# Sample attention with the keys as the stationary operand

## The reference

```python
s = (jnp.einsum('bqhl,bkl->bhqk', q_lat, ckv, preferred_element_type=jnp.float32)
     + jnp.einsum('bqhr,bkr->bhqk', q_pe, kpe, preferred_element_type=jnp.float32))
s = jnp.where(mask, s * MLA_SCALE, NEG_INF)
p = jax.nn.softmax(s, axis=-1).astype(ckv.dtype)
return jnp.einsum('bhqk,bkl->bqhl', p, ckv)
```

## Time and profile before

| what | us |
|---|---|
| median of three timed executions | 4370.94 |
| the profiled execution | 4382.27 |
| its span | 4380.6 |
| PE busy in the span | 3606.5 |
| `mla_sample`, first layer (792 to 1279) | 487 |
| `mla_sample`, second layer (2946 to 3428) | 482 |

### The profile page before, as it was taken

How to read it: one execution, slowest core, us unless ns; L and a number is a source line. 1 busy time by engine, 2 the same in 40 slices (tenths; PEclk the granted TensorE clock), 3 DMA queues, 4 the chain that set the end, 5 groups by cost and what they waited for, 6 DMA issues and landing times. The chain is left out here.

```text
span 4380.6 us, 51760 instructions
## 1 busy us (share of the span) xinstructions
PE 3606.5 (82%) x20008; PEld 3033.2 (69%) x20008; DVE 1946.7 (44%) x3586; ACT 909.6 (21%) x1552; POOL 309.5 (7%) x366
## 2 busy tenths in 40 slices
PE   6974688566688999999999557875677889999997
PEld 4632466455577999999856234654555879999996
DVE  2453666333343544544451646652333344454443
ACT  2013233222221211111111032321222121111112
POOL 2000000222200000000010000003222000000000
PEclk9986799788898999999999658987898999999999
DMA  4111100333310111111121101004222111111111
GB/s 91 25 23 28 28 4 1 99 96 96 94 41 21 54 44 44 58 38 50 24 43 31 28 8 28 4 21 127 89 78 73 39 41 49 44 59 40 49 34 51
DMA packets 227424, 207.29 MB, mean 47 GB/s; under 512 B 51252, under 2 KB 196788, under 8 KB 227012
## 3 DMA queue, kind: packets, MB, share of 16 engines
q1 hardware_dynamic: 200584, 119.11, 10.1%
q0 software_dynamic: 26624, 85.11, 6.7%
HBM read 193.31 MB, written 11.05 MB: 47 GB/s over the span
## 5 line engine op out<-in xcount | busy, mean ns | idle before, releaser
L185 PE MATMUL ps<-streamH,upH 128*128 128x344 f32 x2112 | 451.4, 322 | 36.0 <-DVE streamL L2041 29.7
L185 PE MATMUL ps<-streamH,upL 128*128 128x344 f32 x2112 | 449.1, 321 | 0.0
L185 PE MATMUL ps<-streamL,upH 128*128 128x344 f32 x2112 | 447.6, 320 | 0.0
L185 PEld LDWEIGHTS ps<-streamH,upH 128*128 128x128 f32 x2112 | 356.0, 189 | 40.7 <-issue 34.7
L173 PE MATMUL ps<-hc,wring 128*128 128x344 f32 (+1 forms) x1248 | 366.5, 457 | 21.0 <-DVE hc L410 21.0
L1570 PE MATMUL ps<-kH,qpart 128*128 128x512 f32 x256 | 137.7, 538 | 287.5 <-DVE kL L1682 183.2
L185 PEld LDWEIGHTS ps<-streamH,upL 128*128 128x128 f32 x2112 | 357.7, 189 | 0.0
L185 PEld LDWEIGHTS ps<-streamL,upH 128*128 128x128 f32 x2112 | 354.3, 189 | 0.0
L173 PEld LDWEIGHTS ps<-hc,wring 128*128 128x128 f32 (+1 forms) x1248 | 230.3, 185 | 156.1 <-issue 44.2
L2088 DVE TENSOR_TENSOR xT<-xT,ps 128x1032 f32<-128x1032 f32 x176 | 216.1, 1229 | 240.2 <-PE ps L185 240.2
L1982 ACT ACTIVATE upH<-hc 128x1024 fp32r<-128x1024 f32 x88 | 93.3, 1062 | 981.1 <-PE ps L185 981.1
(11 more groups left out here) (423 smaller groups left out, 5603.1 us busy)
## 6 DMA issues: line engine op xcount, KB each, us to landing
hc<-in_w_ffn_in SPq DMA_DIRECT2D x88, 512.0 KB
hc<-in_w_ffn_out SPq DMA_DIRECT2D x44, 512.0 KB
wring<-in_w_in SPq DMA_DIRECT2D x22, 512.0 KB, 3.9
stream_raw<-in_w_out SPq DMA_DIRECT2D x16, 512.0 KB, 3.9
big<-in_x_prompt SPq DMA_DIRECT2D x1, 4096.0 KB
out_y_prompt<-big SPq DMA_DIRECT2D x8, 512.0 KB
scratch_y<-hc SPq DMA_DIRECT2D x16, 136.0 KB
scratch_u<-wring SPq DMA_DIRECT2D x4, 516.0 KB
```

The costliest lines, as they stand in the source:

```text
L185: last = pe.matmul(self.ps[:, bank + n, 0:NCOL], w, x[:, n * NCOL:(n + 1) * NCOL], start=(k == 0 and i == 0), stop=(k == len(terms) - 1 an ...
```

## The change

`mla_sample` is written anew. Gathers bring the same pages into the same two slots, but a group is now the 1024 keys of four samples, in two halves of the samples by turns; there are 16 groups a layer as before. The latents are still transposed (`latent`), now evicted once as plain fp32, by ACT for even and DVE for odd tiles, into four buffers `KT_`. In `scores` the transposed keys are the stationary operand and the sample's eight query columns move, so that scores stand with keys on the partitions: 128 partitions by 256 columns (sample, tile of keys, head). Rotary scores have 32 moving columns (`rotary_scores`), with the rotary rows transposed straight from `RB`. The softmax runs over 128 lanes, (sample, one of four tiles, head), each with its own running maximum and sum: PE turns the scores (`turned`), DVE takes the maximum along each lane, PE spreads its negative over all partitions by a product with ones (`lowered`), DVE adds it and ACT takes the exponential in place of keys (`pT`). In `values` the rows of `KB` are stationary and eight columns of `pT` move; ACT copies the result, and PE turns it back and sums the probabilities (`back`). After the last group the lanes are merged by their maxima with selecting products. Loops over groups are unrolled in the code of every engine. The sample's own row is handled as a lane of its own. Of the diff, lines that are removed, buffers, the start and the merge are left out here.

```diff
+        def place(g):
+
+            n, z = g // 2, g % 2
+            return n % 2, n // 2, [4 * z + i for i in range(4)]
+
+        def lanes(c, i, j=None):
+            a = c * P + i * 32
+            return slice(a, a + 32) if j is None else slice(a + 8 * j, a + 8 * j + 8)
...
+                for n in range(GATHERS):
+                    slot = n % 2
...
+                        if n >= 2:
+                            g = 2 * (n - 2) + b // 4
+                            pool.wait_ge(f_v, 4 * g + b % 4 + 1)
+                        at = bass.IndirectOffsetOnAxis(self.idx_i[:, n, b:b + 1].bitcast(U32), 0)
                         pool.indirect_dma_start(KB[slot][b], None, ckv_rows, at).then_inc(f_k[slot][b], 16)
                         pool.indirect_dma_start(RB[slot][:, b, :], None, krope_rows, at).then_inc(f_k[slot][b], 16)
...
+                def rotary(g, r):
+                    slot, turn, samples = place(g)
+                    for b in samples[2 * r:2 * r + 2]:
+                        pe.wait_ge(f_k[slot][b], 32 * turn + 32)
+                    if g or r:
+                        pe.wait_ge(f_rte, 2 * g + r)
+                    for x in range(4):
+                        b, c = samples[2 * r + x // 2], x % 2
+                        last = pe.transpose(ps[:, 3, x * P:(x + 1) * P], RB[slot][:, b, c * P:(c + 1) * P], ident)
+                    last.then_inc(f_rt, 1)
+
+                def latent(g, q):
+                    slot, turn, samples = place(g)
+                    b, c, at = samples[q // 2], q % 2, 8 * g + q
+                    pe.wait_ge(f_k[slot][b], 32 * turn + 32)
+                    if at >= KBANKS:
+                        pe.wait_ge(f_ke[(at - KBANKS) % 2], (at - KBANKS) // 2 + 1)
+                    for j in range(4):
+                        last = pe.transpose(ps[:, at % KBANKS, j * P:(j + 1) * P], KB[slot][b][:, (4 * c + j) * P:(4 * c + j + 1) * P], ident)
+                    last.then_inc(f_kt, 1)
+
+                def rotary_scores(g):
+                    samples = place(g)[2]
+                    pe.wait_ge(f_rte, 2 * g + 2)
+                    if g >= 2:
+                        pe.wait_ge(f_sc, g - 1)
+                    for i in range(4):
+                        for c in range(2):
+                            keys = rtb[g % 2][:, (2 * i + c) * P:(2 * i + c + 1) * P]
+                            last = pe.matmul(ps[:, 4 + g % 2, lanes(c, i)], keys, qrb[:, samples[i] * 32:samples[i] * 32 + 32],
+                                             start=(i == 0 and c == 0), stop=False)
+                    last.then_inc(f_rs, 1)
+
+                def scores(g, q):
+                    i, c, at = q // 2, q % 2, 8 * g + q
+                    b = place(g)[2][i]
+                    pe.wait_ge(f_ke[at % 2], at // 2 + 1)
+                    for j in range(4):
+                        last = pe.matmul(ps[:, 4 + g % 2, lanes(c, i, j)], KT_[at % KBUFS][:, j * P:(j + 1) * P], q_of(b),
+                                         start=False, stop=(q == 7 and j == 3))
+                    last.then_inc(f_s, 1)
+
+                def turned(g):
+                    pe.wait_ge(f_sc, g + 1)
+                    if g >= 2:
+                        pe.wait_ge(f_oc, g - 1)
+                    for c in range(2):
+                        last = pe.transpose(ps[:, 6, c * P:(c + 1) * P], raw[g % 2][:, c * P:(c + 1) * P], ident)
+                    last.then_inc(f_mt, 1)
+
+                def lowered(g):
+                    pe.wait_ge(f_dg, g + 1)
+                    pe.matmul(ps[:, 6, 0:P], ones, diag[g % 2], start=True, stop=True).then_inc(f_nm, 1)
+
+                def values(g, i):
+                    slot, _, samples = place(g)
+                    if i == 0:
+                        pe.wait_ge(f_p, g + 1)
+                        if g >= 1:
+                            pe.wait_ge(f_oe, g)
+                    for j in range(4):
+                        for c in range(2):
+                            keys = KB[slot][samples[i]][:, (4 * c + j) * P:(4 * c + j + 1) * P]
+                            last = pe.matmul(ps[:, 7, lanes(0, i, j)], keys, pT[g % 2][:, lanes(c, i, j)],
+                                             start=(i == 0 and j == 0 and c == 0), stop=(i == 3 and j == 3 and c == 1))
+                    last.then_inc(f_v, 1)
+
+                def back(g):
+                    pe.wait_ge(f_oe, g + 1)
+                    pe.wait_ge(f_sb, min(g + 2, GR))
+                    if g >= 1:
+                        pe.wait_ge(f_oc, g)
+                    for c in range(2):
+                        pe.matmul(ps[:, 6, 384:385], pT[g % 2][:, c * P:(c + 1) * P], ones[:, 0:1], start=(c == 0), stop=(c == 1))
+                    pe.transpose(ps[:, 6, 256:384], osb[g % 2], ident).then_inc(f_ob, 1)
...
+                for g in range(GR + 1):
+                    more, late = g < GR, g >= 1
+                    if more:
+                        rotary_scores(g)
+                    for q in range(8):
+                        if more:
+                            scores(g, q)
+                            nxt = 8 * g + q + KBANKS
+                            if nxt < 8 * GR:
+                                latent(nxt // 8, nxt % 8)
+                        if late:
+                            if q == 0:
+                                turned(g - 1)
+                            if q == 2:
+                                lowered(g - 1)
+                            if q == 4 and g >= 2:
+                                back(g - 2)
+                            if q in (4, 5, 6):
+                                values(g - 1, q - 4)
+                            if q == 6:
+                                values(g - 1, 3)
+                        if g + 1 < GR and q in (4, 6):
+                            rotary(g + 1, q // 2 - 2)
+                back(GR - 1)
...
+                def key(at):
+                    act.wait_ge(f_kt, at + 1)
+                    if at >= KBUFS:
+                        act.wait_ge(f_s, at + 1 - KBUFS)
+                    act.activation(KT_[at % KBUFS], ps[:, at % KBANKS, :], ACT.Copy).then_inc(f_ke[0], 1)
+
+                def scores(g):
+                    act.wait_ge(f_s, 8 * g + 8)
+                    act.activation(raw[g % 2], ps[:, 4 + g % 2, 0:256], ACT.Copy).then_inc(f_sc, 1)
+
+                def exponentials(g):
+                    act.wait_ge(f_dg, g + 1)
+                    if g >= 2:
+                        act.wait_ge(f_oc, g - 1)
+                    act.activation(alpha[g % 2], m[g % 2][1 - g // 2 % 2], ACT.Exp, bias=nb[g % 2], scale=MLA_SCALE)
+                    act.wait_ge(f_sb, g + 1)
+                    if g >= 2:
+                        act.wait_ge(f_ob, g - 1)
+                    act.activation(pT[g % 2], raw[g % 2], ACT.Exp, scale=MLA_SCALE).then_inc(f_p, 1)
+
+                def output(g):
+                    act.wait_ge(f_v, 4 * g + 4)
+                    if g >= 2:
+                        act.wait_ge(f_ob, g - 1)
+                    act.activation(osb[g % 2], ps[:, 7, 0:P], ACT.Copy).then_inc(f_oe, 1)
...
+                def maxima(g):
+                    new, old = m[g % 2][g // 2 % 2], m[g % 2][1 - g // 2 % 2]
+                    dve.wait_ge(f_mt, g + 1)
+                    if g >= 2:
+                        dve.wait_ge(f_p, g - 1)
+                        dve.wait_ge(f_nm, g - 1)
+                    dve.reduce_max(mx, ps[:, 6, 0:256], AX).then_inc(f_mx, 1)
+                    dve.wait_ge(f_mx, g + 1)
+                    s.link(TS(new, mx, old, None, ALU.max))
+                    TS(nb[g % 2], new, -MLA_SCALE, None, ALU.mult)
+                    TS(diag[g % 2], ident, new, -1.0, ALU.mult, ALU.mult).then_inc(f_dg, 1)
+
+                def lower(g):
+                    dve.wait_ge(f_nm, g + 1)
+                    both = raw[g % 2].rearrange("p (c x) -> p c x", c=2)
+                    TT(both, both, ps[:, 6, 0:P].unsqueeze(1).to_broadcast([P, 2, P]), ALU.add).then_inc(f_sb, 1)
...
```

More of the change, by code:

```diff
@@ L1459, in mla_sample @@
[L1459 to L1466, removed]
@@ L1581, in values @@
-                def values(i, n):
-                    g, slot, k, half, _ = place(i, n)
-                    pe.wait_ge(f_pte, g + 2)
-                    pe.wait_ge(f_oc, g + 1)
-                    for b in range(SAMPLES):
-                        for j in range(KEYS_GROUP):
-                            key = KEYS_GROUP * half + j
-                            last = pe.matmul(ps[0:64, 7, 0:P], own(pTp[:, j, :], b), KB[k][b][:, key * P:(key + 1) * P],
-                                             start=(b == 0 and j == 0), stop=(b == SAMPLES - 1 and j == KEYS_GROUP - 1))
-                        last.then_inc(f_pv, 1)
@@ L1591, in _ @@
[L1591 to L1602 removed]
+                pe.wait_ge(f_sd, 1)
@@ new lines, in _ @@
+                pe.transpose(ps[0:8, 6, 0:64], px, ident[0:64, 0:64])
+                for z in range(2):
```

(50 more changed lines are left out.)

322 lines of the change are left out of this document (113 added, 209 removed).

## The result

The changed kernel takes 4795.99 us, median of 4 runs (4794.57 to 4797.8), beside 4371.81 us for the kernel before in the same comparison (4 runs, 4367.86 to 4373.24): a ratio of 1.097, 95% interval 1.0955 to 1.0985. It is slower by 424 us where 545 were forecast, inside the range. The profiled execution took 4794.57 us with a span of 4792.9, 412.3 above the span of before.

The account below looks back on a forecast made before the run. PE was taken to bound the kernel. Per layer 10 + 659 (groups) + 75 (gathers) + 13 = 757 us against 487 and 482, together +545: median 4916 us, range for 8 in 10 4500 to 5090.

Parts of the forecast that it names:

- The mechanism: Sample stage: PE stays full, but pairs moving eight columns get a 1.2 GHz clock, 213 ns a pair.
- Rival C: Sample stage: the clock holds at 2.4 GHz, 489 us a layer, 4380 us in all; chance 0.08 together with rival E.
- rival B: Sample stage: the clock goes up in parts, half at each level, 623 us a layer, 4648 us; chance 0.12.
- rival E: Scores stay bound by evictions or the softmax chain, 22.3 us a group; chance 0.08 together with Rival C.
- The price of a group: PE's work on one group of keys: 193 pairs at 0.2135 us, 41.2 us; 16 groups, 659 us a layer.
- The gathers: Page transfers in the sample stage: each of eight costs PE 9.4 us, 75 us a layer, bounds 0 and 120.
- eight dips: Expected sign in the sample stage: PE dips at the gathers, each shorter than 14 us.
- The lower bound, 0: Gathers cost PE nothing, as releases by sample spread the transfers and a slow PE doesn't feel them.
- rival D: Sample stage: clock holds and gathers no longer stop PE, 369 us a layer, 4140 us; chance 0.10.
- Front and end: Sample stage: 10 us to the first transposes, and 13 us at the end, with bounds 8 and 18.
- The added waits: New waits between PE, DVE and ACT sit under PE's work: cost nil; without cover 32 us a layer.

Follow-up runs that it names:

- e2_wide64: The changed kernel with the score matmuls moving 64 columns, zeros beside the sample's eight query columns: 4538.52 us, one run.
- e1: The changed kernel with each score matmul moving 128 columns, 120 of them adding zeros: 4293.89 us, ratio 0.9826 to the kernel before.
- e10: e1 with value products spread one sample to a step, and each layer's second gather released sample by sample: 4236.78 us, ratio 0.9679 to the kernel before.
- e4: The changed kernel with only the first two gathers of each layer, later groups reusing their pages: 4797.04 us, one run.
- e7: The kernel before without the gathers after the second of each layer: 4188.05 us, one run, beside 4371.18.
- e5: e1 with each gather's 16 DMAs issued in one burst after all eight samples of the slot are used: 4481.98 us, one run, beside 4385.09.

## Why the prediction was right, and where its sizes were off

**The mechanism, right.** A group is full of PE (40.00 of 40.00 us), at 0.50, with load durations at the 333 ns that were named beforehand, and DVE and ACT idle most of the time. Rival C (the clock holds), rival B (half at each level) and rival E are excluded by the windows; B came true for 64 columns (e2_wide64: a clock of 0.67), not for eight. That the width of the moving operand is the cause, and not some other part of the new order of work, was only argued from the earlier trace rows in the prediction; e1, with nothing else changed, shows it.

**The price of a group, nearly right.** Forecast 193 x 0.2135 = 41.2 us, measured 40.0, with the count of pairs as forecast. That is 40.0 / 193 = 0.207 us a pair, between the 0.196 and 0.214 of the distances above.

**The gathers, mis-sized.** This is the step that failed: "8 x 9.4 = 75 us a layer". Measured are about 19, all in one place. The stage divides in this way: 15.4 us to the first rotary scores at 806.4; 45.2 the first group; 39.0 the second; 14 of 40.0 to 1450.6; the last values to 1465.4; the end 14.0. From 806.4 to 1465.4 are 659.0 us, by chance just the 16 x 41.2 of the sum: two errors cancel there, the work of PE took 640 us and the loss to the gathers is already in them. The loss is that of the first group alone: while the first two gathers follow each other for 40 us, PE is busy 25.9 of 45.2 us, 19.3 lost. (That these gathers are the cause is shown at the wide setting, by e10.) The other six cost nothing (e4), and of the eight dips that were to show at the gathers only this one came. The sum took the loss as a property of "any moving transfer", from rows in which every transfer was a burst. The lower bound, 0, named the right reason (releases by sample spread the transfers), and that half of rival D came true while its other half, the clock, did not. e1 has both halves for most of the stage, and its 437 and 423 us still stand 68 and 54 above rival D's 369: the first group takes 40.9 us instead of 21.6, later ones up to 25.5 where the clock falls, and the 64 value pairs behind the last group 13.7 us at 0.50:

```profile
1200.56 13.66 PE L1597 MATMUL ps<-wring,big 128*128 128x8 f32 x64
```

So rival D's 4140 us was out of reach even with the clock up in most groups: e1 stands at 4294.

**Front and end.** Forecast 10 and 13, measured 15.4 and 14.0: the first rotary scores need four samples' pages, not one. Per layer then 757 - 75 + 5.4 + 1 = 688.4, the measured stage. Twice 688.4 less 969 is 407.8, and 4.5 us lie elsewhere in the span.

**The added waits**, costed at nothing, cost nothing: PE has no hole in a group. At the full clock they still fit (PE busy for 22.40 of 22.40 us in e1's group), which was also forecast.

The Trainium skill ("TensorE: Matmul & The Clock Gate", "Why this matters for your kernels") ties the full clock to an engine that is kept busy without gaps. This case's windows disagree: 40.00 of 40.00 us busy at a clock of 0.50, and in e1, as busy and 16 times as wide in its scores, at 1.00.

## What to carry to other kernels

Before making the large operand the stationary one, price the load at the clock that thin matmuls get, from a row in the profile that has that very shape (load 128x128, move 8): here 213 ns a pair, not 110. If the pairs are bound by their loads, try the moving operand widened with zeros: 128 columns cost no time here beside the load of a 128 x 128 operand, and turned +9.7% into -1.8%. Release gather buffers in small pieces, and keep two gathers from following each other; the kernel before loses 183 us to its later gathers (e7, one run), and a fine release alone would be worth trying there (it was not tried).

## What the runs showed that was not expected

- More columns made a matmul stream faster: 8 and 32 columns in the scores 40.0 us a group, 64 columns 30.7 once the groups have settled (24 to 40 in the first ones), 128 columns 21.7 to 25.5, and 21.3 to 22.9 with the value products spread.
- A run of transfers without a break holds back PE's completions, by 14 to 15 us for 16 DMAs at once, while PE itself has the work done (900.76 against 916.09 in e5). Ten DMAs at once hold them back by 6 to 7 us (e10). The same bytes in pieces of two DMAs hold back nothing (e4 beside the changed kernel). Why, stays open; no run here tells the causes apart.
- The price of a burst depends on PE's clock: 5.4 to 6.6 us at 0.50, 14.5 to 18.2 with the full clock, in which the clock's own fall is contained.
- Open as well is whether wider value products would remove the last falls of the clock, and whether a pause between the second and the third gather would give back e10's third group; neither was tried.
